# The second column block of an output projection, computed as seven half-size products instead of directly

## What is computed

```python
mix = jnp.concatenate([y_a, y_b], axis=-1)
out = jnp.einsum('bse,ed->bsd', mix, w_out[layer])   # 512 x 2048 times 2048 x 2048
h = h + _rmsnorm(out, post_norm_gain[layer])         # norm over each row of out, gain, residual
```

## Time and profile before

| | us |
|---|---|
| median of 3 runs | 715.9 (715.43 to 716.0) |
| the profiled execution: its own time | 715.07 |
| its span in the trace | 713.2 |
| TensorE busy | 704.1 (99%) |
| weight loads busy | 607.5 (85%) |
| VectorE busy | 587.3 (82%) |
| ScalarE busy | 439.8 (62%) |
| GpSimd busy | 76.1 (11%) |

### The profile page before, as it was taken

The page is one execution under the profiler, slowest core; times in us unless marked ns, Lnnn a source line. Parts: engine busy times, 40 slices in busy tenths (PEclk is TensorE's granted clock), DMA queues, the critical chain, the costliest instruction groups (busy, mean ns, idle before and its releaser), DMA issues.

```text
span 713.2 us, 9845 instructions
## 1 busy us (share of the span) xinstructions
PE 704.1 (99%) x3696; PEld 607.5 (85%) x3696; DVE 587.3 (82%) x756; ACT 439.8 (62%) x598; POOL 76.1 (11%) x94
## 2 busy tenths in 40 slices
PE   8999999999999999999999999999999999999995
PEld 7888888888888888888888888888888888888884
DVE  3499977998789898898897978898898984376787
ACT  4765576666776756777766677766688434253561
POOL 0000000210020110011120011030000000001001
PEclk9999999999999999999999999999999999999999
DMA  8965446567756666656765665656654308467985
GB/s 292 392 199 140 128 118 174 152 171 199 177 117 178 159 194 177 168 145 161 193 156 159 178 173 165 165 147 176 170 168 177 119 24 242 119 176 221 273 331 236
DMA packets 38542, 128.57 MB, mean 180 GB/s; under 512 B 4320, under 2 KB 5344, under 8 KB 37600
## 3 DMA queue, kind: packets, MB, share of 16 engines
q1 hardware_dynamic: 31440, 102.78, 42.1%
q0 software_dynamic: 6912, 25.17, 20.7%
q10 hardware_dynamic: 144, 0.01, 0.0%
HBM read 123.74 MB, written 4.19 MB: 179 GB/s over the span
## 4 chain that ended last, share of the span: by engine, by line
PE 96%; DVE 2%; issue 0%; POOL 0%; DVEq 0%; ACT 0%; ACTq 0%
PE ps L1931 36%; PE ps L1939 19%; PE ps L1875 11%; PE ps L1842 9%; PE ps L1843 9%; PE ps L1841 9%; PE ps L1975 1%; PE ps L1974 1%; DVE mix L1733 1%; PE ps L1907 1%; DVE mix L1635 0%; PE ps L1858 0%; PE ps L1866 0%; PE ps L1868 0%; DVE mix L1663 0%
## 5 line engine op out<-in xcount | busy, mean ns | idle before, releaser
L1931 PE MATMUL ps<-a_ops,w_hi 128*128 128x512 f32 x1120 | 270.8, 391 | 0.0
L1931 PEld LDWEIGHTS ps<-a_ops,w_hi 128*128 128x128 f32 x1120 | 205.6, 188 | 39.4
L674 ACT ACTIVATE w_hi<-raw 128x1024 fp32r<-128x1024 f32 x155 | 163.2, 1055 | 64.7 <-PE ps L1931 35.6
L1147 DVE TENSOR_TENSOR raw_lo<-raw,w_hi 128x1024 fp32r<-128x1024 f32 x155 | 188.8, 1224 | 17.1 <-ACT w_hi L674 16.8
L1939 PEld LDWEIGHTS ps<-a_ops,raw_lo 128*128 128x128 f32 x1120 | 145.7, 191 | 6.3
L1939 PE MATMUL ps<-a_ops,raw_lo 128*128 128x256 f32 x1120 | 149.9, 283 | 0.0
L1788 POOL DMA_DIRECT2D raw<-w_heads x40 | 34.9, 873 | 313.6 <-DMA raw<-w_heads 248.2
L1841 PE MATMUL ps<-w_hi,a_ops 128*128 128x512 f32 x160 | 62.4, 390 | 0.0
L1843 PE MATMUL ps<-w_hi,a_ops 128*128 128x512 f32 x160 | 62.3, 390 | 0.0
L1842 PE MATMUL ps<-raw_lo,a_ops 128*128 128x512 f32 x136 | 53.0, 390 | 0.0
L1162 DVE TENSOR_TENSOR raw<-raw 128x1024 f32<-128x1024 f32 x40 | 48.7, 1218 | 1.0 <-PE ps L1843 1.0
(11 more groups left out here) (232 smaller groups left out, 1027.8 us busy)
## 6 DMA issues: line engine op xcount, KB each, us to landing
raw<-w_heads SPq DMA_DIRECT2D x100, 512.0 KB, 4.2
raw<-w_heads POOLq DMA_DIRECT2D x40, 512.0 KB, 5.7
raw<-w_out SPq DMA_DIRECT2D x35, 512.0 KB, 5.1
raw<-w_v SPq DMA_DIRECT2D x15, 512.0 KB, 10.1
x_rows<-x SPq DMA_DIRECT2D x6, 1024.0 KB, 12.0
mix<-xT SPq DMA_DIRECT2D x16, 256.0 KB, 10.0
out<-mix SPq DMA_DIRECT2D x8, 512.0 KB, 2.7
raw_more<-w_out SPq DMA_DIRECT2D x6, 512.0 KB, 7.6
```

The source lines that it names most:

```text
L674: act.activation(hi_slot(g), raw_slot(raw, slot), ACT.Copy).then_inc(w_hi_done, 1)
L1147: dve.tensor_tensor(raw_slot(raw_lo, slot), raw_slot(raw, slot), hi_slot(g).bitcast(F32), ALU.subtract).then_inc(w_split, 1)
L1931: mm = pe.matmul(dst, hi[:, k * P:(k + 1) * P], a_ops[:, a:a + SEQ], start=k == 0 and p in (0, 1, 5), stop=stop and k == KH - 1, skip_grou ...
```

## The change

Block 1 is computed by the same seven-product form, with halves of 256 columns. `LATE` gets 14 steps "A" in place of 8 plain ones, ahead of the 28 steps that are now called "B". A step of A takes a 128x1024 weight piece as four feature tiles of 256 columns: 2 token tiles x 4 feature tiles x 3 = 24 matmuls of 256 columns, into one bank for both token tiles. The third operand (`s3`) is made during steps 0 to 3. Keeps, joins, squares and gains of A are spread over the loops; the five column pieces (512, 256, 256, 512, 512) have five partial sums of squares a row. B itself keeps its steps, and its product 2 waits for all gains of A.

```diff
-LATE = [("plain", q) for q in range(2 * PAIRS)]
-LATE += [(p, q) for q in range(PAIRS) for p in (0, 1, 2, 6)]
-LATE += [(4, 0), (4, 1), (3, 0), (4, 2), (4, 3)] + [(3, q) for q in range(1, PAIRS)]
-LATE += [(5, q) for q in range(PAIRS)]
+PARTS = {"A": PAIRS // 2, "B": PAIRS}
+LATE = [("A", 0, 0), ("A", 0, 1)]
+LATE += [("A", p, q) for q in range(PARTS["A"]) for p in (1, 2, 6)]
+LATE += [("A", p, q) for p in (4, 5, 3) for q in range(PARTS["A"])]
+LATE += [("B", p, q) for q in range(PAIRS) for p in (0, 1, 2, 6)]
+LATE += [("B", p, q) for p, q in ((4, 0), (4, 1), (3, 0), (4, 2), (4, 3), (3, 1), (3, 2), (3, 3))]
+LATE += [("B", 5, q) for q in range(PAIRS)]
...
+        A_BANK = {0: 0, 2: 0, 5: 0, 1: 1, 3: 1, 6: 2, 4: 3}
...
+            def a_keep_of(p):
+
+                if p in (0, 2):
+                    act.wait_ge(late_done, late_end("A", p) + 1)
+                    if p == 0:
+                        act.wait_ge(s_summed, 5 * PAIRS)
+                    act.activation(a_rows(p // 2, A0), by_token_tile(a_bank(p)), ACT.Copy).then_inc(a_kept, 1)
+                else:
+                    act.wait_ge(a_joined, 1)
+                    act.activation(a_rows(1, A1), by_token_tile(a_bank(1)), ACT.Copy,
+                                   scale=-1.0).then_inc(a_kept, 1)
...
-                if PAIRS <= t < 2 * PAIRS:
-                    s3_hi_of(t - PAIRS)
-                if t == FORM:
-                    for s in range(TT):
-                        rows_square(s, 1)
...
+                if t == late_end("A", 0) + 1:
+                    a_keep_of(0)
+                if t < PAIRS:
+                    s3_hi_of(t)
+                if t == late_end("A", 2) + 1:
+                    a_keep_of(2)
+                if t == late_end("A", 6) + 1:
+                    a_keep_of(1)
+                if t == late_end("A", 4) + 1:
+                    for tile in A_SECOND:
+                        rows_square(*tile)
+                if t == late_end("A", 3) + 1:
+                    for tile in A_FIRST:
+                        rows_square(*tile)
...
+                g, p, q = LATE[t + 2]
+                if p == 1:
+                    late_sum(g, 2, q)
+                if p == 2:
+                    late_sum(g, 6, q)
...
-                if PAIRS <= t < 2 * PAIRS:
-                    s3_lo_of(t - PAIRS)
-                if t == FORM:
-                    for s in range(TT):
-                        rows_gain(s, 1)
+                if t < PAIRS:
+                    s3_lo_of(t)
+                if t == late_end("A", 2) + 1:
+                    a_join_h()
+                if t == late_end("A", 6) + 1:
+                    a_join_f()
+                if t == late_end("A", 4) + 1:
+                    a_join_second()
+                if t == late_end("A", 5) + 1:
+                    a_join_c11()
+                    for tile in A_SECOND:
+                        rows_gain(*tile)
+                if t == late_end("A", 3) + 1:
+                    for tile in A_FIRST:
+                        rows_gain(*tile)
...
+            def a_join_second():
+
+                dve.wait_ge(late_done, late_end("A", 4) + 1)
+                dve.wait_ge(a_joined, 2)
+                dve.wait_ge(a_kept, 3)
+                f, g, p4 = a_rows(1, A0), a_rows(1, A1), by_token_tile(a_bank(4))
+                dve.tensor_tensor(f, p4, f, ALU.add).then_inc(a_joined, 1)
+                dve.tensor_tensor(g, g, p4, ALU.subtract).then_inc(a_joined, 1)
...
-            for q in range(PAIRS):
-                add_late(1, q)
-            for q in range(PAIRS):
-                add_late(4, q)
+            for g in PARTS:
+                for p in (1, 4):
+                    for q in range(PARTS[g]):
+                        add_late(g, p, q)
...
+            def a_step(t):
+
+
+                _, p, q = LATE[t]
+                pe.wait_ge(late_split, SPLIT_AT[t] + 1)
+                if q == 0:
+                    if p == 1:
+                        pe.wait_ge(s_split, 2 * PAIRS)
+                    if p == 2:
+                        pe.wait_ge(s_split, 2 * PAIRS)
+                        pe.wait_ge(a_kept, 1)
+                    if p == 3:
+                        pe.wait_ge(s_split, 3 * PAIRS)
+                        pe.wait_ge(a_kept, 3)
+                    if p == 4:
+                        pe.wait_ge(s3_split, PAIRS)
+                        pe.wait_ge(y_free, HEADS)
+                    if p == 5:
+                        pe.wait_ge(a_kept, 2)
+                for i in range(2):
+                    for k in range(KC):
+                        cols = slice(k * HALF, (k + 1) * HALF)
+                        mm = three(a_tile(p, i), form_operand(p, KC * q + k, i),
+                                   (late_hi(t)[:, cols], late_raw(t, True)[:, cols]),
+                                   p in (0, 1, 4, 5, 6) and q == 0 and i == 0 and k == 0,
+                                   p in (2, 3, 4, 5, 6) and q == PARTS["A"] - 1 and k == KC - 1)
+                mm.then_inc(late_done, 1)
+
+            def b_step(t):
...
                     if p == 2:
-                        pe.wait_ge(rows_free, TT + 2)
-                    if p == 6:
-                        pe.wait_ge(rows_free, 2 * TT)
+                        pe.wait_ge(rows_free, rows_count(*A_FIRST[-1]))
+                    if p in (2, 6):
+                        pe.wait_ge(a_joined, 5)
```

More of the change, by code:

```diff
@@ L103, with late_end @@
 QUADRANTS = P // QUADRANT
+COLUMNS = ((0, BANK), (BANK, BANK + HALF), (BANK + HALF, 2 * BANK), (2 * BANK, 3 * BANK), (3 * BANK, D))
+BLOCKS = len(COLUMNS)
+A0, A1, B0, B1 = range(1, BLOCKS)
+def late_end(g, p):
+    return LATE_OF[g, p, PARTS[g] - 1]
 def step_of(u, p):
@@ L374, in hybrid_layer @@
         late_summed = sem("late_summed")
-        late_t1 = [sem(f"late_t1_{q}") for q in range(PAIRS)]
-        late_t3 = [sem(f"late_t3_{q}") for q in range(PAIRS)]
+        late_t1 = {(g, q): sem(f"late_t1_{g}{q}") for g in PARTS for q in range(PARTS[g])}
+        late_t3 = {(g, q): sem(f"late_t3_{g}{q}") for g in PARTS for q in range(PARTS[g])}
+        a_kept = sem("a_kept")
+        a_joined = sem("a_joined")
         kept = sem("kept")
@@ L429, in late_raw, with late_weights_of, late_place @@
             return (raw_last_lo if lo else raw_last)[:, :]
-        def out_weights_of(dc, q):
+        def late_weights_of(g, col, half, q):
+            if g == "A":
+                chunk = w_out[KK + half * PARTS["A"] + q].rearrange("p (k c) -> p k c", k=KC)
+                return chunk[:, :, col * HALF:(col + 1) * HALF]
+            q += half * PAIRS
             a = q % 2 * QUARTER
-            return w_out[KK * dc + q // 2][:, a:a + QUARTER]
+            return w_out[KK * (2 + col) + q // 2][:, a:a + QUARTER]
+        def late_place(t):
+            raw_t = late_raw(t)
+            return raw_t.rearrange("p (k c) -> p k c", k=KC) if LATE[t][0] == "A" else raw_t
         def tail_rows(s, a, b):
@@ L440, in late_base @@
         def late_base(t):
[L441 to L444, removed]
+            g, p, q = LATE[t]
+            return late_weights_of(g, int(p in (2, 3, 4)), int(p not in (0, 1, 4)), q)
+        SUMS = {("A", q): 2 * q + 1 for q in range(PARTS["A"])}
+        SUMS.update({("B", q): 2 * (PARTS["A"] + q) + 1 for q in range(PAIRS)})
         OP_AT = {1: 4, 2: 5, 3: 6}
@@ L1714, in _ @@
                     late_lo_of(t + 2 + PAIRS)
-            for n in range(4):
-                rows_gain(*FORM_TILES[n])
+            for tile in B_SECOND:
+                rows_gain(*tile)
             row_mean(2)
@@ L1720, in row_final @@
                 n = ROW_ORDER.index(s)
-                for dc in range(TT):
+                for dc in range(BLOCKS):
                     dve.wait_ge(rows_free, rows_count(s, dc))
@@ L2045, in rows_tile @@
                     tile = OUT_KK[c] * KC + k
-                    mm = three(rows_bank(dc, s), both((mix_part(tile, 0), mix_part(tile, 1)), s * P, (s + 1) * P),
+                    mm = three(rows_bank(s), both((mix_part(tile, 0), mix_part(tile, 1)), s * P, (s + 1) * P),
                                both((hi, lo), k * BANK, (k + 1) * BANK),
@@ L2137, in form_step @@
                 form_tile(t, 1).then_inc(late_done, 1)
-            for t in range(FORM):
-                plain_step(t)
-            for t in range(FORM, LAST):
-                form_step(t)
+            for t in range(LATE_OF["B", 0, 0]):
+                a_step(t)
+            for t in range(LATE_OF["B", 0, 0], LAST):
+                b_step(t)
             pe.wait_ge(kept, 2)
```

250 lines of the change are left out of this document (130 added, 120 removed).

## The result

The changed kernel takes 721.55 us (median of 6 runs, 720.32 to 721.66), the kernel before 715.58 us on the same chip (6 runs, 714.75 to 716.0): ratio 1.0081, interval 1.007 to 1.0092. That is slower, as forecast, but by 5.8 us (0.0081 of 715.6) in place of 1.8, and outside the range of 715.6 to 720.2. The profiled execution took 721.37 us, its span is 719.6; before, 715.07 and 713.2. So 6.4 us of span have to be found.

A forecast was written before the change was run, and what follows sets the result against it. TensorE, busy 704.1 of 713.2 us, was taken to bound the kernel. The terms -3.4 + 1.8 + 2.9 + 0.5 = +1.8 us gave 716.9 us for the profiled execution, 717.7 on the median; range 715.6 to 720.2.

The forecast's parts named there:

- The price of the small matmuls: New block on TensorE: 336 matmuls of 256 columns at 119.4 ns, 40.1 us in place of 43.5, saving 3.4 us.
- The first stall: Before step 2 of the new block TensorE waits 1.8 us for VectorE's rest, queued behind late_sum and the post gain.
- The second stall: Before step 3 of the new block TensorE waits 2.9 us for ScalarE's copy a_keep_of(0), queued behind a rounding.
- The border stall: At the next block's product 2, which waits for all eight gains: a stall of 0.5 us, bounded by 0 and 1.2.
- The clock: Rival, chance 0.08: after TensorE's two pauses a stretch at the 1.2 GHz level loses 2.2 us, giving 719.9 us.
- the means over five partials: Means taken over five partial sums in place of four: claimed to cost nothing that a row shows.
- the blocks behind are the same instructions: Blocks after the changed one: claimed unchanged, so the shift of +1.75 us at step 16 carries to the end.
- The transfers: 14 loads and 4 accumulating ones for 8 loads in the new block: 33.7 us in 44 us, cost 0.
- The chance of slower, 0.56: Whole kernel: probability given to a time slower than before by more than 0.2%.

The follow-up runs named there:

- the reordered kernel: Changed kernel with tiles at their old addresses, product 0's copy ahead of chunk 4's rounding, gains, squares and s3 spread over later steps: 712.76 us, ratio 0.9963 to before.
- the kernel with the fillers: Changed kernel with tiles at their old addresses, plus 20 unread 256-column matmuls ahead of step 3's wait: 716.78 us, ratio 1.0023 to the kernel before.
- the one with its tiles as before: Changed kernel with out_ms and out_rstd sharing one tile, so later tiles lie at their old addresses: 718.12 us, ratio 1.0037 to the kernel before.

## Why the prediction was wrong

By its own steps, against the profile after:

- **The price of the small matmuls held.** 120.0 ns from start to start against 119.4; 336 of them 40.3 us against 40.1. Term -3.4, measured -3.2. The gap formula of the Trainium skill (TensorE: Matmul & The Clock Gate, Back-to-back issue gap), which the page calls that of an isolated matmul, gave 109.2 ns; the trace does not agree.
- **The first stall held.** +1.8 predicted, 1.5 us measured (594.74 would have been the next slot after the last of step 1, 596.27 it was), released by VectorE's rest, as said.
- **The second stall held.** +2.9 predicted, 2.8 us measured, released by ScalarE's copy, as said. That both are caused by the order of the two queues is shown by the reordered kernel, in which 0.4 us of them are left.
- **The border stall did not come.** +0.5 predicted within 0 to 1.2, measured 0: the last gain ends at 640.46 and product 2's first matmul follows its predecessor at 640.69 without a gap, just in time (0.23 us from result to matmul, 0.25 were counted). The slow stretch is not the reason: the kernel with the fillers has none and no pause at the border either. From the first matmul of step 10 it is 16.75 us to the end of the last gain and 16.98 to product 2 there (618.92, 635.67, 635.90), and 16.74 and 16.97 in the changed kernel (623.72, 640.46, 640.69). The forecast had 17.1 and 16.9 (619.2, 636.3, 636.1). So the chain through ScalarE's squares and VectorE's queue was counted 0.35 us too long.
- **The clock was given 0.08 and came.** The prediction had the mechanism and its cause right and priced it at 2.2 us from the kernel's start; 15 slow matmuls cost 1.4 us. With the stalls the block comes to -3.2 + 1.5 + 2.8 + 0 + 1.4 = +2.5, measured 2.71. The step that was wrong here is the weight: I read "no row of before shows a pause in mid-kernel" as a reason against. It was absence of evidence, and the two stalls that I forecast myself were just such pauses. The Trainium skill (TensorE: Matmul & The Clock Gate, What's actually happening) calls the throttled state the default, which activity releases; this trace is in line with that (0.50 after pauses of 1.5 and 2.8 us with one step of 24 matmuls between).
- **The step that failed** is the sentence that the means over five partials "cost nothing that a row shows", and with it "the blocks behind are the same instructions" and a block that starts at 585.78. I read the wider tile as arithmetic and not as an allocation. It was worth 3.1 us, more than any stall of the sum, and by itself in the kernel before 3.9 us; nothing in the sum or the rivals had a place for it. Removing it alone gives 718.1 us, 0.4 us from the 717.7 of the forecast. That this is so near is in part luck: it holds the 1.4 us of the clock, which the sum lacked, while the two pauses are 0.4 us shorter than forecast and the border stall of 0.5 us is missing.
- **The transfers cost nothing,** as forecast: the queues' shares rose from 42.1 and 20.7% to 43.3 and 22.4%, and no wait of TensorE behind the block is in the list.

The chance of slower, 0.56, was on the right side. The range missed by 1.3 us because the sum had no term for what the change does to the stages ahead of the block.

## What to carry to other kernels

When an edit changes the size or number of SBUF tiles, compare the addresses of every matmul operand behind them before anything else: here a tile that is 16 bytes wider cost more than the edit it came with could earn. Before a block gets shorter steps, write out what the queues of VectorE and ScalarE hold ahead of its first weights, and spread what has no due time (gains, squares, later operands) over later steps; that turned +0.37% into -0.37% here. Price a pause of TensorE with the half-speed stretch behind it, not with its own length alone.

## What the runs showed of the hardware

- The SBUF address of an operand changed the pace of matmuls of 512 columns with fp32r operands. In the values stage and in the last chunk of block 0 they took 226.7 ns from start to start with all operands 128 bytes past a multiple of 256, and 233 ns when x (the stationary operand) or o_hi3 and o_lo3 (the moving one) lay 32 bytes up or down or 128 down; with 64 bytes down it was 229 ns in the values stage and 233 to 234 in the chunk of o_hi3. It is no rule for all: the products of q and k took 234 ns at the first place and 227 ns 32 bytes up. The Trainium skill (SBUF — State Buffer, Operand start alignment) has an operand start at any multiple of its element size and says that the runs behind this timed nothing; these addresses were all legal, and the price here is 3% of each matmul that pays it.
- Matmuls of 256 columns in the new block did not change, 120 ns in both the changed kernel and the one with its tiles as before, but for 16: those with raw_more_lo took 123 ns in the first. The 8 of q_hi and k_hi took 118 ns in the kernel before and 128 ns 32 bytes up.
- The granted clock fell to 0.50 in mid-kernel after TensorE had been idle for 1.4 and 2.7 us with one step of 24 matmuls between. The slow matmuls began 0.8 us into the step behind the second pause (0.35 us with the tiles as before), and the clock was back at 1.00 some 3 us of work later. With 1.7 and 2.1 us idle it fell too; with 1.2 and 0.3 us, or with 0.4 alone, it did not.
